# A two-block transformer step in fp32 on one core: the joints between stages, reordered by token tile

## The reference, cut to what matters

```python
# first block, layers i = 0, 1
h = layer_norm(ALPHA * h + mixer(h), ln1_g[i], ln1_b[i])
h = layer_norm(ALPHA * h + square(relu(h @ mlp_w1[i])) @ mlp_w2[i], ln2_g[i], ln2_b[i])
h = h + sigmoid(h @ ple_gate_w[i]) * (p[i] @ ple_w[i])       # gate times embedding projection
# second block, layers l = 0, 1
x = x + 0.5 * swiglu(rmsnorm(x, norm_ffn1[l]), ...)
x = x + hybrid_mixer(rmsnorm(x, norm_mix[l]), ...)
x = x + 0.5 * swiglu(rmsnorm(x, norm_ffn2[l]), ...)
# at the end
return rmsnorm(x, norm_final)
```

## Time and profile before

| | |
|---|---|
| runs | 4071.73, 4076.27, 4077.88 us |
| profiled execution | 4077.22 us, its span 4075.2 us |
| mean granted clock of TensorE | 0.953 of full |
| busy: PE, DVE, ACT, POOL | 3785.0, 1903.4, 1428.9, 135.8 us |
| weight queue (q1) | 300.85 MB, 21.0% of the 16 engines' span |

### The profile page before, as it was taken

How to read it: one execution, slowest core, us unless ns; L and a number is a source line. 1 busy time by engine, 2 the same in 40 slices (tenths; PEclk the granted TensorE clock), 3 DMA queues, 4 the chain that set the end, 5 groups by cost and what they waited for, 6 DMA issues and landing times.

```text
span 4075.2 us, 44964 instructions
## 1 busy us (share of the span) xinstructions
PE 3785.0 (93%) x17824; PEld 3076.7 (75%) x17824; DVE 1903.4 (47%) x2696; ACT 1428.9 (35%) x2041; POOL 135.8 (3%) x118
## 2 busy tenths in 40 slices
PE   8999699989998998899979988999999989899998
PEld 6766588867667887688867687888788767687886
DVE  4445744445735444333357464333333366463333
ACT  3323232225534322332254343322322253443322
POOL 0000000000200000000000130000000000310000
PEclk9979799989998998999999999999999999899999
DMA  4000122222012222222221011222222221012221
GB/s 166 32 32 32 52 93 98 99 80 86 22 52 83 94 103 79 81 95 102 84 73 45 21 53 59 97 94 93 93 94 93 85 73 45 1 63 83 96 101 57
DMA packets 43696, 303.72 MB, mean 75 GB/s; under 512 B 4960, under 2 KB 5216, under 8 KB 8928
## 3 DMA queue, kind: packets, MB, share of 16 engines
q1 hardware_dynamic: 43488, 300.85, 21.0%
HBM read 298.74 MB, written 2.10 MB: 74 GB/s over the span
## 4 chain that ended last, share of the span: by engine, by line
PE 83%; DVE 11%; ACT 4%; issue 1%; DMA 0%; DVEq 0%; ACTq 0%; SPq 0%
PE ps L403 80%; DVE arena L1761 3%; PE ps L412 3%; ACT arena L1016 2%; DVE arena L1765 2%; DVE split L1761 1%; DVE X L1761 1%; ACT L1016 1%; ACT split L1016 1%; DVE arena L1757 1%; DVE small L1777 1%; DVE X L1765 0%; DVE arena L1789 0%; DMA X<-in_x 0%; DVE split L1765 0%
## 5 line engine op out<-in xcount | busy, mean ns | idle before, releaser
L403 PE MATMUL ps<-split 128*128 128x512 f32 (+1 forms) x13212 | 3111.0, 395 | 41.9 <-DVE split L1761 17.6
L403 PEld LDWEIGHTS ps<-split 128*128 128x128 f32 x13212 | 2491.4, 190 | 591.7 <-issue 53.2
L1761 DVE TENSOR_TENSOR split<-ring,split 128x1024 fp32r<-128x1024 f32 (+1 forms) x554 | 674.6, 1218 | 1450.9 <-ACT split L1016 1438.6
L1016 ACT ACTIVATE split<-ring 128x1024 fp32r<-128x1024 f32 (+1 forms) x554 | 582.3, 1051 | 1465.7 <-PE ps L403 1447.9
L403 PE MATMUL ps<-arena 128*128 128x128 f32 (+9 forms) x3344 | 517.4, 310 | 65.9 <-ACT arena L1016 12.4
L403 PEld LDWEIGHTS ps<-arena 128*128 128x128 f32 (+2 forms) x3344 | 420.1, 200 | 143.3 <-issue 76.4
L1016 ACT ACTIVATE arena<-ps 128x512 f32<-128x512 f32 (+4 forms) x540 | 280.7, 520 | 432.7 <-PE ps L403 256.1
L412 PE MATMUL ps<-C,arena 128*128 128x128 f32 (+4 forms) x764 | 134.1, 318 | 87.9 <-DVE arena L1757 52.0
L412 PEld LDWEIGHTS ps<-C,arena 128*128 128x128 f32 (+4 forms) x764 | 110.1, 171 | 107.4 <-issue 84.0
L1761 DVE TENSOR_TENSOR arena<-arena 128x512 f32<-128x512 f32 (+5 forms) x246 | 145.8, 593 | 63.6 <-ACT split L1016 49.5
L1761 DVE TENSOR_TENSOR arena<-arena,ps 128x512 f32<-128x512 f32 x192 | 132.0, 687 | 72.7 <-PE ps L403 51.9
(11 more groups left out here) (99 smaller groups left out, 1077.4 us busy)
## 6 DMA issues: line engine op xcount, KB each, us to landing
ring<-in_wts SPq DMA_DIRECT2D x268, 1024.0 KB, 4.8
ring<-in_wts SPq DMA_DIRECT2D x19, 512.0 KB, 3.4
X<-in_x SPq DMA_DIRECT2D x1, 2048.0 KB, 12.7
out<-arena SPq DMA_DIRECT2D x4, 512.0 KB, 2.7
C<-in_cb SPq DMA_DIRECT2D x1, 2003.5 KB, 8.2
ring<-in_wts SPq DMA_DIRECT2D x2, 784.0 KB, 4.3
ring<-in_wts SPq DMA_DIRECT2D x2, 576.0 KB, 10.0
ring<-in_wts SPq DMA_DIRECT2D x2, 256.0 KB, 2.7
```

Of the source, the lines that this page charges most:

```text
L403: return e.matmul(out, l, r, start=start, stop=stop, skip_group_check=True)
L1016: o.sig(a.activation(out, i, f, **kw), sig)
L1761: o.sig(v.tensor_tensor(out, a, b, op), sig)
```

## The change

The four parts of a joint no longer run one after the other over all tokens but token tile by token tile, and overlap with the linears at both sides.

- **`last`**: the last two pieces of a linear before a joint run tile by tile (both pieces for token tile 0, then for 1, ...). Into this, transposes of tiles 0 and 1 are put at the places in `slots`.
- **`first`** (joints before a feature-major linear: up00, up10, gu10.., h0, gu20..): the first two pieces of the next linear run in two column halves of 256 tokens: half 0 of pieces 0 and 1, then half 1. `mid` says where tiles 2 and 3 are transposed.
- A token tile is transposed into two banks (g = 0, 1: feature tiles 0 to 3, 4 to 7), so `H` is filled by tile j and half g.
- Banks: the linear with `last` and the one with `first` use banks 0 to 3 ("lin"), the linear before and the transposes 4 to 7 ("side").
- Layer norm: per tile two passes on DVE, (x - mean) * weight row and (...) * 1/std + bias row; ScalarE does only the root. The statistics of the first feature half are taken with the residual add of the linear before (`half_stats`).
- RMS norm: squares of the first feature half beside the last linear (`half_squares`), of the second half in the joint, a root per tile on ScalarE, and one pass on DVE, x * 1/rms * weight row. Six weight rows (512 KB each) are loaded for it, earlier in the order of loads; the gains as columns go.
- Embedding: pw0 and pw1 run before pg0 and pg1, in the layer-norm joint; ScalarE copies their results to SBUF; `pT` is split during dn31.
- The first rows of the norm weights (`ln1`, `ln2`) are loaded before the joint.

```diff
@@ plan: rows loaded earlier; pw before pg (the same for e_out, o_out, wo and fd with their rows)
+        load(f"ln2{l}", f"ln2_{l}", 0, 1, 0, 2048)
         for c in range(2):
-            lin(f"pg{l}{c}", ...)
             lin(f"pw{l}{c}", f"pw_{l}", 2, c * 512, 512, False)
+        for c in range(2):
+            lin(f"pg{l}{c}", f"pgw_{l}", 8, c * 512, 512, False, between=[("gfx10", "g1_0", 0, 1, 0, 1024)] if (l, c) == (1, 1) else ())
@@ TensorE
+    def tile(L, p, m, src, cols, of):
+        ...
+        for k in range(p.c):
+            kk = p.k + k
+            if kk == 0 and cols.start == 0:
+                bank(L.name, m, of=of)
+        ...
+    def lin(name, src, ready=None, ms=range(4), mix=None, each=None, of=None, last=None, first=None):
+        of = of or ("lin" if last or first or mix is not None else "all")
+        if first:
+            for u in range(2):
+                for x, p in enumerate(ps[0:2]):
+                    first(u, x)
+                    if u == 0:
+                        e.wait_ge(S["lo"], p.i + 1)
+                    for m in ms:
+                        i = tile(L, p, m, src, slice(256 * u, 256 * u + 256), of)
+                        ...
+        ...
+        if last:
+            for m in ms:
+                for x, p in enumerate(ps[-2:]):
+                    ...
+                    close(L, p, m, tile(L, p, m, src, whole, of), ms)
+                    last(m, x)
+    def joint(name, src, ok, slots, mid):
+        def turned(j):
+            e.wait_ge(*ok(j))
+            for g in range(2):
+                b = bank(name, j, g, of="side")
+                for f in range(4):
+                    x = tr(b.t[:, f * 128:(f + 1) * 128], src[:, j, (4 * g + f) * 128:(4 * g + f + 1) * 128])
+                full(b, x)
+        def last(m, x):
+            for j in slots.get((m, x), ()):
+                turned(j)
+        def first(u, x):
+            for j in mid.get((u, x), ()):
+                turned(j)
+            if x == 0:
+                for j in (2 * u, 2 * u + 1):
+                    e.wait_ge(*emptied(name, j, 0))
+    rms: slots = {(3, 0): [0], (3, 1): [1]} if name == "fx10" else {(2, 0): [0], (3, 0): [1]}; mid = {(0, 1): [2, 3]}
+    ln:  slots = {(2, 1): [0], (3, 1): [1]}; mid = {(1, 0): [2, 3]}
@@ mlp_ple, TensorE
+            lin(f"pw{l}{c}", K.m.pT, ..., of="lin")
+            J2.turned(2 + c)
+        lin(f"pg{l}0", H, each=J2.each, of="side")
+        lin(f"pg{l}1", H, last=J3.last)
@@ ScalarE
+    def half_squares(added):
+        for m in range(4):
+            a.wait_ge(*added(m))
+            act(K.n.xn[:, m, 0:512], X[:, m, 0:512], ACT.Square, "jn_a" if m == 3 else None, accum_out=r0[:, m:m + 1])
+            yield
+    def rms_root(j, added):
+        a.wait_ge(*added(j))
+        act(K.n.xn[:, j, 0:512], X[:, j, 512:1024], ACT.Square, accum_out=r1[:, j:j + 1])
+        if j == 0:
+            told("jn_d")
+        act(r1[:, j:j + 1], r1[:, j:j + 1], ACT.Sqrt, "jn_a", scale=1.0 / 1024, bias=r0[:, j:j + 1])
+    rms_join: split(p[0]), flush, two gates (fx10), root 0, root 1, turned(0), two gates (fx10),
+              turned(1, g 0), root 2, turned(1, g 1), root 3, split(p[1]), turned(2), turned(3)
+    mlp_ple:  root 0, root 1, turned(0), turned(1), split(pw1), root 2, projected(0), root 3, turned(2),
+              prime(pg0), projected(1), turned(3)
@@ DVE
+    def ln_scaled(j, key):
+        stt(x, x, ag[:, j, 0:1], g, ALU.subtract, ALU.mult)
+        told("jn_a")
+        recip(rs[:, j:j + 1], rs[:, j:j + 1])
+        stt(x, x, rs[:, j:j + 1], bt, ALU.mult, ALU.add, "ln_x")
+    def ln_join(name, key, splits):
+        split(splits[0])
+        for j in (0, 1):
+            next(side)                 # res_add of tile j, its statistics
+            ln_scaled(j, key)
+        for j in (0, 1):
+            turned(name, j)
+        split(splits[1])
+        for j in (2, 3):
+            next(side)
+            ln_scaled(j, key)
+        for j in (2, 3):
+            turned(name, j)
+    rms_join: split(p[0]), sums of half 0; add 0, scaled(0), add 1, scaled(1) (fx10: adds first), turned(0),
+              add 2, add 3, turned(1, g 0), scaled(2), turned(1, g 1), scaled(3), split(p[1]), turned(2), turned(3)
+    at the end: half_summed(); for j in range(4): next(side); rms_scaled(j, nfin, "done")
```

More of the change, by code:

```diff
@@ L35 @@
     NCB += _w
+JOINS = ("fx10", "hx0", "fx20", "fx11", "hx1", "fx21")
 class Bag:
@@ new lines, in joint @@
+    def joint(name, src, ok, slots, mid):
+        J = Bag()
+        def turned(j):
[14 more added lines that the diff above has]
+                    e.wait_ge(*emptied(name, j, 0))
+        J.turned, J.last, J.first = turned, last, first
+        J.ready = lambda k: [emptied(name, j, 1) for j in range(4)] if k == 4 else []
+        J.each = lambda kk, m: emptied(name, m, kk // 4)
+        return J
@@ new lines, in rms_join @@
+    def rms_join(name, then, added, gate=none):
+        p = lins[then].pieces
+        split(p[0])
+        flush()
+        next(gate, None)
+        next(gate, None)
+        rms_root(0, added)
+        rms_root(1, added)
+        turned(name, 0)
+        next(gate, None)
+        next(gate, None)
+        turned(name, 1, (0,))
+        rms_root(2, added)
+        turned(name, 1, (1,))
+        rms_root(3, added)
+        split(p[1])
+        turned(name, 2)
+        turned(name, 3)
+    def mlp_ple(l):
+        nonlocal ucount, side
@@ L1482, in ffn @@
             for c in range(2):
-                lin(f"fd{w}{l}{p}{c}", idle())
+                lin(f"fd{w}{l}{p}{c}", half_squares(lambda m: emptied(f"fd{w}{l}20", m)) if p + c == 2 and p == 2 else idle())
+        added = lambda m: emptied(f"fd{w}{l}21", m)
+        if then:
+            rms_join(name, then, added)
+            return
+        flush()
+        for j in range(4):
+            rms_root(j, added)
     def hybrid(l):
@@ L1494, in hybrid @@
             act(s[:, 2:6], s[:, 2:6], ACT.Exp, "to_dve")
-        def told(what):
-            a.wait_ge(S[what], o.due(what))
         def ev_hg():
@@ L2387, in ffn @@
                 lin(f"fd{w}{l}{p}{c}", res_add(f"fd{w}{l}{p}{c}", None, 0.5, c * 512))
+        if then:
+            rms_join(name, then)
+            return
+        half_summed()
+        for j in range(4):
+            next(side)
+            rms_scaled(j, lins["nfin"], "done")
     def hybrid(l):
```

496 lines of the change are left out of this document (281 added, 215 removed).

## The result

The changed kernel takes **3984.13 us** (median of 4 runs, 3980.39 to 3992.66) where the kernel before, in the same rounds, takes 4076.11 (4071.73 to 4077.88): a ratio of **0.978, interval [0.976, 0.980]**. Forecast were 3976 and a range of 3940 to 4015. The profiled execution took 3984.05 us, its span 3982.2. Two lines of the page answer to the earlier trace rows: busy time, and the chain by line.

The account below looks back on a forecast made before the run. TensorE bounds the kernel, so only its standing time can shrink: joints, stalls and slow first pieces go from 218.7 to 126.4 us (-92.3), the tail -8.7, so 4077.2 - 101.0 = 3976.2; predicted 3976 us, range 3940 to 4015.

Parts of the forecast that it names:

- the embedding stalls: Two TensorE stalls of 3.39 us inside the embedding stages, forecast to go.
- one product takes a bank: A product takes a bank that its forerunner has just used: +1 us.
- fx10: RMS-norm joint behind the gates, with three table loads for one: 12.4 us where 19.82 stood.
- five RMS joints: Joints hx0, fx20, fx11, hx1, fx21: 9.2 us lost each, 46.0 together where 80.6 stood, with 4.9 behind them.
- tail: From the last matmul to the end: 9.3 us instead of 18.01, a gain of 8.7.
- Column halves at 0.128 us: Price of a 256-column matmul in the first two pieces behind a joint: +1.4 us in each of eight joints.
- Layer norm before the MLPs: Two joints: 13.8 us lost plus 3.2 for the clock, 34.0 together where 21.94 and 22.03 stood.
- Layer norm before the gates: Two joints, gap filled by embedding projections: 12.3 us lost plus 2 for the clock, 28.6 together.
- RMS: Each of five RMS joints: loss 8.2 us at the full clock, plus 1.0 for the clock.
- A: Rival: joints stop longer and the clock falls, half the gain is given back, some 4020 us; chance 0.20.
- C: Rival: slower, column-halved pairs and transposes keep the clock at 1.2 GHz through the joints, 4094 us; chance 0.04.
- B: Rival: the clock never falls in the joints and a half matmul costs half, 3948 us; chance 0.12.

Follow-up runs that it names:

- aligned banks: Changed kernel, but after the first product behind a joint the bank rotation starts on banks 4 to 7 wherever it would start on 0 to 3: 3978.09 us, ratio 0.976.
- after: The changed kernel itself, with the whole change, against the kernel before: 3984.13 us, ratio 0.978; run again unaltered, 3986.72 us, ratio 0.977.

## Why the prediction was right, and where it was not

The time came out 8 us (0.2%) above the forecast, and part of this closeness is luck. The joints and the tail gave 82.8 us where 100.9 were forecast, 18 us too few; 10.2 us came from a first stage that happened to be short in the profiled run, and for which the forecast had nothing. With the first stages alike, the change gives 84 us and the time is some 3992: inside the range, 16 us above the forecast. Grouped as in its sum, with the ends of the last matmul ahead of each joint from the two timelines:

| group | forecast us | measured us |
|---|---|---|
| four layer-norm joints and the embedding stalls | -39.8 | -27.6 |
| "one product takes a bank": +1 | +1.0 | +1.5 and +9.4, inside the layer-norm and the RMS number |
| into the odd mixer, and fx10 | -13.9 | -12.6 |
| five RMS joints | -39.5 | -34.3 |
| tail | -8.7 | -8.3 |
| sum of these (the rest) | -100.9 | -82.8 |
| first stage | 0 | -10.2 |

- *TensorE bounds, DVE's chain decides in the joints:* right. Every stop named was there, most within 0.3 us.
- *Column halves at 0.128 us:* right (0.130). By the formula of the Trainium skill, "TensorE: Matmul & The Clock Gate", section "Back-to-back issue gap", an isolated one would take 109 ns; in this trace, where each follows a weight load, it takes 130.
- *Layer norm before the MLPs:* stops of 10.4 us at the first joint against 7.8; those ahead of the transposes of tiles 0 and 1 (1.18 and 1.01) were not foreseen, as DVE's chain takes 4.9 us a tile and not 4.6. The clock cost 2.8 us there (30 and 50 half matmuls in 5.24 and 7.96 us, at 0.13 each), 3.2 were added. At the second such joint the stops are 7.5 us, and the clock cost 4.3 (18 and 30 half matmuls in 4.08 and 6.44 us).
- *Layer norm before the gates:* under-sized. Stops of 9.5 us at the first (1.01, 1.47, 3.21, 3.79) against 7.7 (1.3, 3.3, 3.1), and 3.1 for the clock against 2; at the second 8.8 and some 3.
- *RMS:* 8.2 us were right, and the 1.0 for the clock was not needed: in five joints with stops up to 1.63 us it did not fall.
- *"One product takes a bank that its forerunner has just used: +1":* the step that failed. There were two such places, and 9.4 us stood at one. I had looked at the order of the pools in the code, not at where the rotation stands when each joint is reached: the first product of the last feed-forward starts at bank 1, so that the next one waits for the bank emptied last, 5.58 us, and then the clock falls. The run with aligned banks shows it. Without these 9.4 us the RMS joints would have given 43.7, more than forecast.
- *fx10:* right, 7.1 us won against 7.4. What precedes the stop was three table loads and the order of the queues; on ScalarE after:

```profile
1623.87 1.28 ACT L1091 ACT_TABLE_LOAD   x1
1625.16 0.29 ACT L1091 ACTIVATE small<-small 128x1 f32<-128x1 f32 x1
```

 The next instruction starts 0.01 us behind the load. The 1.38 us of drain that the Trainium skill, "ScalarE: Activation LUTs", section "What ACT_TABLE_LOAD costs", adds to each switch are not in this trace either.
- *Rivals:* A (half given back) and C (slower) had the right place, the clock behind long stops, and too high a price: it fell at all layer-norm joints and at fx10, not at the five RMS joints. B's premise (it never falls) is wrong.
- *Its signs of being wrong:* 24 half matmuls took 3.12 us (over 3.4 was the sign), and no DMA releases TensorE behind a joint. But the mean clock is 0.969 and 0.967 in the two profiles, not above 0.97: this sign did show. It fits the places where the forecast fell short, the clock behind the layer-norm joints and behind the bank stop, though the mean also covers the mixers, which the change leaves alone.
- *Open:* of the 12.2 us by which the layer-norm group fell short these rows place some 10 (2.2, 2.9, 2.3 with the 1.5 of the banks, and 2.5 at the four joints in order of time). The others lie inside stages, where some stretches have two lengths; no run separates them. What decides when the clock falls is open too (see the two stops of 3.21 us).

## What to carry to other kernels

In this kernel a wait that was cut into pieces was still bound by the chain that feeds it: count that chain per tile first, then ask which queue entry can move into its idle time (two weight splits moved ahead of two copies were worth 12 us; reordering the chain itself some 5). Filling a gap paid here only once the next instruction behind it was ready too. Where buffers rotate past work that takes its own, write down where the rotation stands at every entry; and compare two profiles from a row on that the change cannot reach.

## What the runs showed of the hardware

- The same instructions in the first mixer took 431.7 to 447.6 us until one and the same row, in fourteen profiles of fourteen executions. Behind it the stages repeat within 0.1 us from one profile of after to the other. Nearly all of the spread of the runs (3980 to 3996 us for after) can come from there. The idle time in it hardly differs (54 to 58 us); TensorE's mean clock does (0.90 to 0.93).
- In after, TensorE's clock stayed at 1.00 through the stops of 0.73 and 1.63 us of the RMS joints, and was at 0.50 behind stops of 3.79, 4.49 and 5.58 us, for some 5 us of work each. Behind a stop of 3.21 us it was at 1.00 in one joint and at 0.50 in another.
